# Last three slots of a two-layer decoder step: their output rows summed and written by themselves, the last down product in two banks of its own

## The chip, the cores and the metric

The kernel runs on one core of one Trainium2 chip. The metric is the device time of an execution in microseconds; a profiled execution also gives a trace.

## The reference, cut to what matters

A prompt group (512 tokens) and a sample group (64 tokens) go through two layers with shared weights, D = 1024. Each layer has a mixer (chunked gating and differential attention) and then a mixture of experts, which is what the change touches:

```python
def hier_moe(x, g2, r_g, r_e, w_gate, w_up, w_down):
    h = rmsnorm(x, g2).reshape(b * t, d)
    # group by argmax of softmax(h @ r_g); two experts of its four by softmax(h @ r_e)
    gates = ...                       # (tokens, 16), two non-zero
    hg = jnp.einsum('nd,edf->nef', h, w_gate)
    hu = jnp.einsum('nd,edf->nef', h, w_up)
    a = jax.nn.silu(hg) * hu * gates[..., None]
    return jnp.einsum('nef,efd->nd', a, w_down)
xp = xp + hier_moe(xp, ...)           # and the same for xs
```

The results are both x after layer 2, and the new key and value rows of both layers.

## The kernel before

**Tokens.** The tokens are five tiles of up to 128 rows (`NT`; tile `TP` = 4 has the 64 sample rows). Rows lie in `x` (SBUF). `h_rows` (DRAM) holds the normed rows; `y_rows` (DRAM) has 2 x 640 rows of expert results. Of a token's two experts, the one later in the order of places writes into the first 640 rows (main, or "higher"), the other into the second 640 ("lower").

**Slots.** The experts are worked off in 14 slots (`SLOTS`) of 128 token rows; slots 0 to 10 may mix experts, and slots 11, 12, 13 (`LAST` = 11) each hold one expert of the group's last places, so their rows are always main rows. Tokens that don't fit go to extra slots, whose number is read by every engine from `flags` at the end (`extra_slots`, `only_if`); here there are none. A slot n is: POOL gathers rows of `h_rows` (L634); TensorE transposes them (`turn_in`), VectorE scales them (`in_turned`, L1993); TensorE makes the gate and up products in two halves (`up`); ScalarE applies silu (L1375), VectorE multiplies (`gated`, L2007); TensorE turns the result (`turn_act`, bank J) and ScalarE copies it (`act_turned`, L1379); TensorE makes the down product (`down`, banks O, 4 x 2 matmuls of 512 columns); ScalarE copies it to `y_sb` (`result`, L1386); POOL scatters it to `y_rows` (`scatter`, L641).

**Order.** It is written out by hand. TensorE in step n: first half of up(n), turn_act(n-1), second half of up(n), turn_in(n+1), down(n-1). At the end come a flush and the branch on the extra slots. Every engine works its instructions in order, DMA issues too. In POOL's loop the gather of slot n+3 stands ahead of the scatter of slot n. SP issues all weight loads (L480), each when the buffer it takes is free; ten pieces of 1 MB are in SBUF.

**End of a layer.** While slots 12 and 13 run, ScalarE's queue loads the lower rows (`y_low`, L1401) and VectorE adds them to x with their gate (`add_low`, L1999), behind the gated products of these slots. Tokens whose lower row is in an extra slot have gate zero here (`late_gates`). When the scatters of all slots have landed, ScalarE's queue loads the main rows (`y_high`, L1417), VectorE adds them (`add_high`, also L1999), and in layer 1 SP stores x to the outputs (L498). In layer 0 TensorE does matmuls without use meanwhile (`keep_busy`, L713), 30 of them, of two passes each. The next layer starts with the transposes of x (`turn_input`, L695) and VectorE's scaling of them (L1473).

## Time and profile before

| | us |
|---|---|
| median of 3 runs (lowest, highest) | 998.91 (998.38, 1002.36) |
| profiled execution | 999.48 |
| its span | 997.8 |
| TensorE busy in it | 957.9 |
| VectorE, ScalarE, POOL busy | 457.8, 247.0, 193.6 |

The span goes from the first to the last instruction. TensorE is busy 96% of it; the 40 us that it isn't are mostly the end of layer 1 and, less, the end of layer 0. The DMA engines moved 197.5 MB, 198 GB/s over the span.

### The profile page before, as it was taken

Reading aid. Unit: us, or ns where it says so; the run is one execution under the profiler, and the core shown is the slowest. Engines: PE = TensorE matmul, PEld = TensorE weight load, DVE = VectorE, ACT = ScalarE, POOL = GpSimd, SP = SyncE. Lnnn points to the kernel's source line nnn. Section 1 sums busy time; section 2 is a strip of 40 time slices with the busy share of each in tenths; the row PEclk is TensorE's granted clock in tenths of the full one; section 3 lists DMA queues with packets and bytes.
Section 4 is the critical chain, followed back from the end, with each engine's and each line's share of the span. In section 5 each row is a group of like instructions: output and inputs, shape, how many; then the busy total and the mean of one; then the engine's idle time right before and its main releaser. Section 6 shows DMA issues by size and latency. Waiting matters only on the chain.

```text
span 997.8 us, 13511 instructions
## 1 busy us (share of the span) xinstructions
PE 957.9 (96%) x4838; PEld 489.5 (49%) x4838; DVE 457.8 (46%) x1210; ACT 247.0 (25%) x489; POOL 193.6 (19%) x267
## 2 busy tenths in 40 slices
PE   9999999999999999999899999999999999999991
PEld 5444455556456444434544445555565554444340
DVE  2403234676456665551433212456663575555523
ACT  3102355642001111111221124556220012111110
POOL 2333201331101111111124041023220012111100
PEclk9999999999999999999999999999999999999996
DMA  9706003342514979998651150135252168799946
GB/s 347 267 30 263 1 1 132 96 159 83 234 53 138 371 267 369 416 422 320 234 165 58 65 199 1 61 114 167 61 208 116 43 264 327 290 385 413 403 152 222
DMA packets 39769, 197.50 MB, mean 198 GB/s; under 512 B 7652, under 2 KB 7780, under 8 KB 23824
## 3 DMA queue, kind: packets, MB, share of 16 engines
q1 hardware_dynamic: 19456, 136.01, 34.9%
q0 software_dynamic: 15888, 45.79, 13.3%
q10 hardware_dynamic: 4352, 14.76, 4.0%
q8 instruction: 42, 0.69, 0.3%
q14 instruction: 31, 0.25, 0.1%
HBM read 177.22 MB, written 29.88 MB: 208 GB/s over the span
## 4 chain that ended last, share of the span: by engine, by line
PE 87%; DVE 5%; issue 3%; DMA 2%; ACT 1%; POOL 1%; POOLq 1%; ACTq 0%; DVEq 0%
PE ps L697 79%; PE ps L695 7%; DMA cat<-y_rows 1%; DMA y_rows<-hn,isca 1%; DVE cat L1852 1%; PE ps L713 1%; DMA hT<-h_rows,igat 1%; DVE hT L1993 0%; POOLq L526 0%; DVE hT L1473 0%; ACT hn L1386 0%; DVE x L1999 0%; DVE tmp L1559 0%; DVE tmp L1609 0%; POOL st L521 0%
## 5 line engine op out<-in xcount | busy, mean ns | idle before, releaser
L697 PE MATMUL ps<-ring,hT 128*128 128x512 f32 (+2 forms) x1056 | 382.7, 595 | 2.8 <-DVE hT L1473 1.6
L697 PEld LDWEIGHTS ps<-ring,hT 128*128 128x128 f32 (+2 forms) x1056 | 148.6, 166 | 195.5 <-issue 193.8
L697 PE MATMUL ps<-ring,cat 128*128 128x512 f32 (+2 forms) x560 | 195.3, 596 | 2.4 <-ACT hn L1386 2.4
L697 PEld LDWEIGHTS ps<-ring,cat 128*128 128x128 f32 (+2 forms) x560 | 72.9, 162 | 81.7 <-issue 78.8
L641 POOL DMA_INDIRECT y_rows<-hn,isca x28 | 29.2, 1044 | 249.0 <-ACT hn L1386 228.5
L697 PE MATMUL ps<-hT,ring 128*128 128x512 f32 (+1 forms) x256 | 71.8, 437 | 0.9 <-DVE tmp L1559 0.7
L521 POOL TENSOR_TENSOR st<-st,half 128x1 f32<-128x1 f32 (+3 forms) x60 | 63.5, 1058 | 11.3 <-POOL st L519 11.1
L1494 DVE TENSOR_REDUCE st<-sqj 128x8 f32<-128x512 f32 x20 | 13.5, 681 | 111.7 <-ACT sqj L1235 111.6
L519 POOL TENSOR_SCALAR st<-st 128x1 f32<-128x1 f32 (+3 forms) x60 | 15.1, 252 | 238.7 <-DVE st L1494 82.8
L1993 DVE TENSOR_TENSOR hT<-ps,par 128x512 f32<-128x512 f32 x56 | 36.2, 686 | 47.9 <-PE ps L695 47.1
L1386 ACT COPY hn<-ps 128x1024 f32<-128x1024 f32 x28 | 28.4, 1013 | 116.3 <-PE ps L697 116.3
L697 PEld LDWEIGHTS ps<-hT,ring 128*128 128x128 f32 x256 | 38.1, 191 | 30.5 <-issue 28.4
L527 POOL DMA_DIRECT2D kc<-in_ck x32 | 24.6, 770 | 102.3 <-PE ps L697 78.2
L1220 ACT ACTIVATE sqj<-x 128x1024 f32<-128x1024 f32 x10 | 10.6, 1058 | 119.6 <-DVE x L1686 99.1
L1307 ACT ACTIVATE ring<-ps,st 128x128 f32<-128x128 f32 (+3 forms) x64 | 33.2, 524 | 27.1 <-DVE st L1621 26.8
L1887 DVE TENSOR_REDUCE o_sb<-ps 128x4 f32<-128x12 f32 (+2 forms) x18 | 3.0, 164 | 80.1 <-PE ps L697 80.1
L1235 ACT ACTIVATE sqj<-ps,st 128x512 f32<-128x512 f32 (+1 forms) x20 | 13.7, 686 | 97.9 <-PE ps L697 91.3
L697 PE MATMUL ps<-vc,hT 128*128 128x512 f32 (+2 forms) x112 | 36.5, 598 | 0.9 <-issue 0.9
L634 POOL DMA_INDIRECT hT<-h_rows,igat x26 | 26.5, 1019 | 51.1 <-DVE isca L1891 44.9
L1473 DVE TENSOR_TENSOR hT<-ps,g_sb 128x512 f32<-128x512 f32 x20 | 12.9, 686 | 49.4 <-PE ps L695 49.4
L1375 ACT ACTIVATE cat<-ps 128x256 f32<-128x256 f32 x28 | 10.8, 385 | 97.6 <-PE ps L697 97.6
L527 POOL DMA_DIRECT2D vc<-in_cv x32 | 17.7, 552 | 87.9 <-PE ps L697 72.0
(269 smaller groups left out, 1219.4 us busy)
## 6 DMA issues: line engine op xcount, KB each, us to landing
ring<-in_w SPq DMA_DIRECT2D x82, 1024.0 KB, 8.3
kc<-in_w SPq DMA_DIRECT2D x12, 1024.0 KB
vc<-in_w SPq DMA_DIRECT2D x10, 1024.0 KB
v<-in_w SPq DMA_DIRECT2D x10, 1024.0 KB
kva<-in_w SPq DMA_DIRECT2D x10, 1024.0 KB
kc<-in_ck POOLq DMA_DIRECT2D x32, 256.0 KB, 3.7
vc<-in_cv POOLq DMA_DIRECT2D x32, 256.0 KB, 3.3
h_rows<-qk ACTq DMA_DIRECT2D x10, 512.0 KB, 2.6
```

The lines of the kernel that those rows point to most:

```text
L519: nc.gpsimd.tensor_scalar(stat["ms"][at, 0:n], src, 1.0 / size, EPS, ALU.mult, ALU.add).then_inc(*pool_c.inc())
L521: nc.gpsimd.tensor_tensor(dst, stat["ms"][at, 0:n], half[at, 0:n], ALU.pow).then_inc(*pool_c.inc(*label))
L527: pool.dma_start(buffer(b % 2, g), view(d[table][bass.DynSlice(l * NPOOL + page, 1)])).then_inc(*arrived[b % 2].inc("kv", b, by=16))
L634: pool.indirect_dma_start(hs[:, b, :], None, h_rows, bass.IndirectOffsetOnAxis(index, 0), bounds_check=TOK - 1, oob_is_err=False).then_inc ...
L641: pool.indirect_dma_start(rows, bass.IndirectOffsetOnAxis(index, 0), y_sb[:, b, :], None, bounds_check=rows.shape[0] - 1, oob_is_err=False ...
L695: ins = pe.transpose(out, lhsT, rhs)
L697: ins = pe.matmul(out, lhsT, rhs, start=start, stop=stop, skip_group_check=loose)
L1235: nc.scalar.activation(sqj[at, t % 2, :], bank(u)[at, :], ACT.Square, scale=stat["rs"][at, t:t + 1]).then_inc(*act_s.inc("sq", name, t))
L1307: ins = nc.scalar.activation(e_sb[:, n % 2, m, 0:(i + 1) * P], bank(f"S{n % 2}", m)[:, 0:(i + 1) * P], ACT.Exp, bias=stat["nb"][:, c:c + 1 ...
L1386: nc.scalar.copy(y_sb[:, b, :], ps[:, 6:8, :].rearrange("p a n -> p (a n)")).then_inc(*read["O"].inc("down", *key))
L1494: vec.tensor_reduce(stat["ssk"][:, 8 * t:8 * t + 8], groups(sqj[:, t % 2, :], 8, DK), AX.X, ALU.add).then_inc(*dve_s.inc("ss" + name, t))
L1993: vec.tensor_tensor(hsT[:, b, hf * HALF:(hf + 1) * HALF, :], bank(f"T{hf}").rearrange("p (j t) -> p j t", j=HALF), g, ALU.mult).then_inc(* ...
```

## The change

Only in layer 1 (`l == L - 1`):

- SP (`last_rows`), behind all weight loads: stores x to a new DRAM table `x_rows` (five stores), stores for each token a pair of gates to `g_rows` (five small stores), waits for the scatters of slots 9 and 10, loads the five tiles of lower rows to `y_low`, then, when the pieces through down(10) are free, the five tiles of main rows into freed weight buffers; stores each tile of x to the output when its sum is made (`dve_s "sum"`), waits for the three last scatters (`fin_out`), and only then reads the number of extra slots.
- POOL (`final_rows`), between the gather of slot 13 and the scatter of slot 10: waits for `x_rows` and `g_rows` and gathers, for slots 11, 12, 13, the rows of x and the gate pairs (six indirect gathers). Behind the scatter of slot 10 (`lower_rows`): waits for the scatters of 9 and 10 and gathers the three slots' lower rows. The scatters of slots 11 to 13 to `y_rows` are gone (they stand in the branch for extra slots); instead `final_out` scatters the summed rows to the output, after all main stores have landed.
- VectorE: small operations for the gates in slot 5 (`final_gates`); gate zero for main rows that the last slots will write themselves. Behind the gated product of slot 12: wait for `x_rows`, five `add_low`, `add_main` for tiles 0 and 1. Behind that of slot 13: `add_main` for tiles 2 to 4, `slot_lower` and `slot_higher` for the three slots. For slot 13 `slot_higher` reads the down product from PSUM in two halves.
- ScalarE no longer loads `y_low` or `y_high` when there are no extra slots.

In both layers: `turn_act` of slot 13 is done between the two halves of down(12) and ScalarE copies it ahead of the result of slot 12; down(13) goes into banks J and I, and ScalarE copies the halves one by one. `keep_busy` is 32 instead of 30 between the layers, and 5 at the start of both layers instead of 6 at the start of layer 0 alone. The outputs of both groups are one tensor, and at the start one more block of 64 rows of `y_rows` is zeroed.

```diff
+                def last_rows():
+                    for t in range(NT):
+                        sp.dma_start(x_rows[PLACE[t] * P:(PLACE[t] + 1) * P, :], x[:, t, :]).then_inc(*x_kept.inc("x", by=16))
+                    sp.wait_ge(*dve_s.at("pairs"))
+                    for t in range(NT):
+                        sp.dma_start(g_rows[PLACE[t] * P:(PLACE[t] + 1) * P, :], g_pair[:, t, :]).then_inc(*g_kept.inc("g", by=16))
+                    for b in range(2):
+                        sp.wait_ge(*y_out[b].at("y", "m", last_slot(b, LAST)))
+                    for t in range(NT):
+                        sp.dma_start(y_low[:, t, :], y_rows[TOK + PLACE[t] * P:TOK + (PLACE[t] + 1) * P, :]).then_inc(*lower_in[t].inc("early", by=16))
+                    sp.wait_ge(piece_used.sem, l * PER_LAYER + (N_DENSE + FIN_FREE + CREDIT))
+                    for t in range(NT):
+                        n = NROW if t == TP else P
+                        sp.dma_start(y_main(t)[0:n, :], y_rows[PLACE[t] * P:PLACE[t] * P + n, :]).then_inc(*main_in[t].inc("main", by=16))
+                    for t in range(NT):
+                        sp.wait_ge(*dve_s.at("sum", t))
+                        sp.dma_start(d["y"][PLACE[t] * P:(PLACE[t] + 1) * P, :], x[:, t, :]).then_inc(*stored.inc("main", by=16))
+                    sp.wait_ge(*fin_out.at("fin"))
...
+                def final_rows():
+                    wait(*x_kept.at("x"))
+                    wait(*g_kept.at("g"))
+                    wait(*pool_c.at("g_slot"))
+                    for i, n in enumerate(FIN):
+                        for out, table, landed in ((x_slot[n], x_rows, xg_in[i]), (g_slot[:, i, :], g_rows, gg_in[i])):
+                            pool.indirect_dma_start(out, None, table, bass.IndirectOffsetOnAxis(igat[:, n:n + 1], 0),
+                                                    bounds_check=TOK - 1, oob_is_err=False).then_inc(*landed.inc("in", by=16))
+                def lower_rows():
+                    for b in range(2):
+                        wait(*y_out[b].at("y", "m", last_slot(b, LAST)))
...
+                        pool.indirect_dma_start(yg_slot[n], None, y_rows, bass.IndirectOffsetOnAxis(ilow[:, i:i + 1], 0),
+                                                bounds_check=2 * TOK - 1, oob_is_err=False).then_inc(*yg_in[i].inc("in", by=16))
+                def final_out(n):
+                    wait(*dve_s.at("fin", n))
+                    wait(*stored.at("main"))
+                    pool.indirect_dma_start(d["y"], bass.IndirectOffsetOnAxis(igat[:, n:n + 1], 0), x_slot[n], None,
+                                            bounds_check=TOK - 1, oob_is_err=False).then_inc(*fin_out.inc("fin", by=16))
                 for n in range(NSLOT):
                     if n + 3 < NSLOT:
                         gather_main(n + 3)
+                    if l == L - 1 and n == LAST - 1:
+                        final_rows()
...
-                    scatter(n % 2, isca[:, n:n + 1], ("m", n), y_out[n % 2])
+                    if l < L - 1 or n < LAST:
+                        scatter(n % 2, isca[:, n:n + 1], ("m", n), y_out[n % 2])
+                    if l == L - 1 and n == LAST - 1:
+                        lower_rows()
+                if l == L - 1:
+                    for n in FIN:
+                        final_out(n)
...
-                    keep_busy(30, "I")
+                    keep_busy(32, "I")
...
-                                if l == 0:
-                                    keep_busy(6, "I")
+                                keep_busy(5, "I")
...
+                    out = ("J", "I") if key == ("m", NSLOT - 1) else ("O",)
+                    for u in out:
+                        claim(u)
...
+                        if between and c == 0:
+                            between()
...
                     gated(n % 2, ("m", n))
+                    elif n == NSLOT - 2:
+                        dve.wait_ge(*x_kept.at("x"))
+                        for t in range(NT):
+                            add_low(t)
+                        add_main(0)
+                        add_main(1)
+                    elif n == NSLOT - 1:
+                        for t in range(2, NT):
+                            add_main(t)
+                        for work in (slot_lower, slot_higher):
+                            for m in FIN:
+                                work(m)
```

## Rows read from the trace of the kernel before

**Rows 1.** Busy time by stage: start:end, length, engines busy (operations), granted clock, DMA share, GB/s
```profile
core 0: us, PE busy (x) PEld busy (x) DVE busy (x) ACT busy (x) POOL busy (x), PEclk, DMA share, GB/s
900.00:920.00 20.00, 20.00 (x74) 7.94 (x70) 10.24 (x32) 3.15 (x5) 4.05 (x4) 1.00 1.02 414
980.00:998.00 18.00, 0.00 (x0) 0.00 (x0) 6.29 (x5) 0.00 (x0) 0.00 (x0) 0.50 0.76 277
```
**Rows 2.** The chain that ended last, from 961: start, length, what
```profile
973.29 3.69 PE ps L697 x8
...
977.00 1.02 ACT hn L1386
...
978.88 3.44 DMA y_rows<-hn,isca
...
982.39 0.32 ACTq L1417
...
983.71 7.47 DMA cat<-y_rows
...
991.20 1.28 DVE x L1999
```
**Rows 3.** Timeline of slots 12 and 13: start, length, operation [idle before, releaser]
```profile
957.51 1.29 DVE L1993 TENSOR_TENSOR hT<-ps,par 128x512 f32<-128x512 f32 x2 [9.93 <-PE ps L695]
...
968.27 3.60 PE L697 MATMUL ps<-kc,cat 128*128 128x512 f32 x8
...
968.89 0.42 DVE L2007 TENSOR_TENSOR cat<-cat,ps 128x256 f32<-128x256 f32 x1 [9.76 <-ACT cat L1375]
...
973.29 3.67 PE L697 MATMUL ps<-ring,cat 128*128 128x512 f32 x8 [1.20 <-ACT hn L1386]
```
**Rows 4.** SP's last weight issue, SP's waits for landed weights (L163), and that stretch
```profile
939.58 0.33 SPq L480 DMA_DIRECT2D ring<-in_w  x1
...
L163 SPq EVENT_SEMAPHORE  x5: 17/17/17, 953.2 to 953.5; - x5
...
950.00:953.20 3.20, 3.20 (x8) 1.28 (x7) 0.00 (x0) 0.83 (x1) 1.01 (x1) 1.00 0.24 99
```
**Rows 5.** DMA issues of the page: count, KB each, median us from issue to landing
```profile
h_rows<-qk ACTq DMA_DIRECT2D x10, 512.0 KB, 2.6
...
g_sb<-in_g ACTq DMA_DIRECT2D x1, 8.0 KB, 2.4
```
**Rows 6.** Timeline of POOL around the scatter of slot 10
```profile
939.43 1.01 POOL L641 DMA_INDIRECT y_rows<-hn,isca  x1 [9.80 <-ACT hn L1386]
940.74 1.01 POOL L634 DMA_INDIRECT hT<-h_rows,igat  x1 [0.31 <-issue]
951.71 1.01 POOL L641 DMA_INDIRECT y_rows<-hn,isca  x1 [9.96 <-ACT hn L1386]
```
**Rows 7.** Timeline of VectorE, adds of the reloaded main rows (tiles 0, 1; tile 2)
```profile
986.04 2.53 DVE L1999 SCALAR_TENSOR_TENSOR x<-cat,st,x 128x1024 f32<-128x1024 f32 x2 [9.53 <-DMA cat<-y_rows]
...
989.53 1.28 DVE L1999 SCALAR_TENSOR_TENSOR x<-cat,st,x 128x1024 f32<-128x1024 f32 x1 [0.95 <-DMA cat<-y_rows]
```
**Rows 8.** Stretch after the short gaps between the layers (columns as rows 1)
```profile
489.00:492.00 3.00, 3.00 (x18) 3.00 (x17) 0.00 (x0) 0.00 (x0) 0.00 (x0) 0.57 0.19 62
```
**Rows 9.** Timeline from the last down product of layer 0 to the first product of layer 1
```profile
482.07 3.67 PE L697 MATMUL ps<-ring,cat 128*128 128x512 f32 x8 [1.21 <-ACT hn L1386]
...
485.78 1.01 ACT L1386 COPY hn<-ps 128x1024 f32<-128x1024 f32 x1 [3.81 <-PE ps L697]
...
487.88 8.56 PE L713 MATMUL ps<-c 128*128 128x128 f32 x60 [2.03 <-issue]
...
495.17 2.54 DVE L1999 SCALAR_TENSOR_TENSOR x<-cat,st,x 128x1024 f32<-128x1024 f32 x2 [8.26 <-DMA cat<-y_rows]
...
499.18 1.10 PE L697 MATMUL ps<-ring,hT 128*128 128x512 f32 x2 [1.57 <-DVE hT L1473]
```
**Rows 10.** SP's load of the number of extra slots: durations ns, start
```profile
L430 SPq TENSOR_LOAD <-flags x1: 276/276/276, 940.0 to 940.0; - x1
```

More of the change, by code:

```diff
@@ L326, in program @@
         y_outx = [count(f"y_outx{b}") for b in range(2)]
+        x_kept, g_kept, fin_out = count("x_kept"), count("g_kept"), count("fin_out")
+        stored_again = count("stored_again")
+        main_in, lower_in, x_again = ([count(f"{n}_in{t}") for t in range(NT)] for n in ("main", "lower", "x_again"))
+        xg_in, gg_in, yg_in = ([count(f"{n}_in{i}") for i in range(3)] for n in ("xg", "gg", "yg"))
         early_in, low_in, high_in = ([count(f"{n}_in{t}") for t in range(NT)] for n in ("early", "low", "high"))
@@ L343, in program @@
         LOW_AT = {LAST + 1: (0, 1), LAST + 2: (2, 3, 4)}
+        FIN = tuple(range(LAST, NSLOT))
+        assert len(FIN) == 3 and all(len(SLOTS[n]) == 1 and SLOTS[n][0][1:] == (0, P) for n in FIN)
         def last_slot(b, below=NSLOT):
@@ L491, in load @@
                                      ).then_inc(*landed[SLOT[i]].inc("w", i, by=16))
-                extras(sp, n_extra, load, arrivals=landed)
-            for t in range(NT):
-                n = NROW if t == TP else P
-                sp.wait_ge(x_ready.sem, L * NT + t + 1)
-                sp.dma_start(d["ys"] if t == TP else d["yp"][t * P:(t + 1) * P, :], x[0:n, t, :]).then_inc(*stored.inc(by=16))
-            sp.wait_ge(stored.sem, stored.now())
+                extras(sp, n_extra, load, done=store_again if l == L - 1 else None, arrivals=landed, uncounted=[stored_again])
+            sp.wait_ge(*stored.at("main"))
             sp.wait_ge(*v_stored.at("v"))
@@ L637, in scatter @@
                 def scatter(b, index, key, landed):
-                    wait(*read["O"].at("down", *key))
+                    for u in ("J", "I") if key == ("m", NSLOT - 1) else ("O",):
+                        wait(*read[u].at("down", *key))
                     rows = y_rows[0:TOK, :] if key[0] == "m" and key[1] >= LAST else y_rows
-                    pool.indirect_dma_start(rows, bass.IndirectOffsetOnAxis(index, 0), y_sb[:, b, :], None,
+                    result = y_last if l == L - 1 and key == ("m", NSLOT - 1) else y_sb[:, b, :]
+                    pool.indirect_dma_start(rows, bass.IndirectOffsetOnAxis(index, 0), result, None,
                                             bounds_check=rows.shape[0] - 1, oob_is_err=False).then_inc(*landed.inc("y", *key, by=16))
@@ L675, in next_in @@
                         gather(b, rows_at(igat, 2, 0), (key, b), hs_inx[b])
+                    if l == L - 1 and (key, b) == ("e", 0):
+                        for n in FIN:
+                            scatter(n % 2, isca[:, n:n + 1], ("m", n), y_out[n % 2])
                     wait(*read["O"].at("down", key, b))
@@ L1140, in down @@
                             for at, i in parts:
[L1141 to L1142 removed]
+                                u, k = (out[c], 0) if len(out) == 2 else ("O", c)
+                                mm(bank(u, k)[at, :], actT[:, b, f, at], piece(i)[:, f * D + c * W:f * D + (c + 1) * W], start=(f == 0), stop=(f == 1),
+                                   inc=full[u].inc("down", *key) if ((c or len(out) == 2) and f and at.stop == P) else None)
+                        if between and c == 0:
+                            between()
                 def weights(n, part):
@@ L1426, in load_again @@
                     scattered_mains()
+                    if l == L - 1:
+                        act.wait_ge(*stored.at("main"))
+                        for t in range(NT):
+                            act.dma_start(x[:, t, :], x_rows[PLACE[t] * P:(PLACE[t] + 1) * P, :]).then_inc(*x_again[t].inc("x", by=16))
                     for t in range(NT + 2):
@@ new lines, in add_main, with slot_lower @@
+                def add_main(t):
+                    n = NROW if t == TP else P
+                    dve.wait_ge(*main_in[t].at("main"))
+                    vec.scalar_tensor_tensor(x[0:n, t, :], y_main(t)[0:n, :], stat["main"][0:n, t:t + 1], x[0:n, t, :], ALU.mult, ALU.add
+                                             ).then_inc(*dve_s.inc("sum", t))
+                def slot_lower(n):
+                    i = FIN.index(n)
+                    for arrived in (xg_in[i], gg_in[i], yg_in[i]):
+                        dve.wait_ge(*arrived.at("in"))
+                    vec.scalar_tensor_tensor(x_slot[n], yg_slot[n], g_slot[:, i, 1:2], x_slot[n], ALU.mult, ALU.add).then_inc(*dve_s.inc("lower", n))
@@ new lines, in slot_higher @@
+                def slot_higher(n):
+                    i = FIN.index(n)
+                    dve.wait_ge(*dve_s.at("lower", n))
+                    if n < NSLOT - 1:
+                        dve.wait_ge(*read["O"].at("down", "m", n))
+                        vec.scalar_tensor_tensor(x_slot[n], y_sb[:, n % 2, :], g_slot[:, i, 0:1], x_slot[n], ALU.mult, ALU.add).then_inc(*dve_s.inc("fin", n))
+                        return
+                    for c, u in enumerate(("J", "I")):
+                        dve.wait_ge(*full[u].at("down", "m", n))
+                        cols = x_slot[n][:, c * W:(c + 1) * W]
+                        ins = vec.scalar_tensor_tensor(cols, bank(u), g_slot[:, i, 0:1], cols, ALU.mult, ALU.add)
+                    ins.then_inc(*dve_s.inc("fin", n))
```

110 lines of the change are left out of this document (89 added, 21 removed).

## The prediction

> **What bounds the kernel now.** Read first the busy time by stage: until about 970 TensorE is busy all the time at full clock (20.00 of 20.00 us), and in the last stage, 980 to 998, it does nothing while VectorE has 6.29 us of work and the DMA engines are 0.76 busy [rows 1]. So everything up to 970 is worth what TensorE saves, and the last 28 us are worth what their own chain of waits costs. That chain [rows 2]: the last down product starts at 973.29, ScalarE copies it out (977.00), the scatter to y_rows takes until 982.32, the first reload of y_rows is issued at 982.39, the fourth is waited for until 991.18, VectorE adds, x is stored, and the span ends at 997.8. From the copy's end (978.02) that is 19.8 us of moving rows. The timeline of the last two slots shows the second thing: TensorE waits 1.2 us between slots 12 and 13, for bank O and the turned activations, and VectorE, after the gated product of slot 12, sits idle 9.76 us until that of slot 13 at 968.89 [rows 3].
>
> The change takes the 19.8 us apart, and puts into the idle time of VectorE, POOL and the DMA engines around 940 to 969 what has to be ready sooner. The question is whether that fits ahead of the two things it is queued in front of: on POOL the scatter of slot 10, on VectorE the gated product of slot 13, for which TensorE waits. I work in the times of the trace of before.
>
> **Layer 1, x into DRAM.** SP issues the five stores of x after its last weight load, issued at 939.58 [rows 4]. They go behind it in the same queue. SP's own wait for the landing of the last weights is over at 953.2: by then few DMA engines still work (99 GB/s from 950 to 953.2, against 414 in the steady stream), and all 16 must finish each transfer [rows 1, 4]. Each engine has 1/16 of 2.62 MB to go, at 414 GB/s 6.3 us: 959.5. A lone store of 512 KB takes 2.6 us to landing [rows 5], 1.3 of them beyond its bytes; five tiny stores of gates follow. I take 1.0 for both: x and gates are there at 960.5. Lower end: the engines idle from 950 to 953.2 have by then moved (414 - 99) x 3.2 = 1.0 MB of it, 2.4 us less, and nothing for the rest: 957. Upper end: 2.4 us for the tiny stores, as for the lone 8 KB load [rows 5], and stores a fifth slower than loads: 963.5.
>
> The Trainium skill (DMA: Bandwidth & Descriptors, section "Queues, rings and completion order") says that each DMA engine takes one issuer's descriptors in ring order. That is what keeps x behind the weights; the trace agrees in so far as the wait for the last weights ends with the late engines at 953.2; without the rule the lower end, 957 or less, would be the value.
>
> **Layer 1, POOL.** After the gather for slot 13 (940.74) POOL now waits for x and the gates and issues six gathers (x and gates, three slots), and only then the scatter of slot 10. Before, that scatter began at 951.71 [rows 6]. POOL takes 0.9 us from a release to the start of such an operation (copy's end 978.02, scatter 978.88 [rows 2]), and scatter and gather follow one another at 1.31 us. So 960.5 + 0.9 + 6 x 1.31 = 969.3 for the scatter, 17.6 us late, with 3.4 to landing [rows 2] 972.7. Lower end of the six: 1.01 each, the operation alone, 6.1; upper end: 1.31, as nothing here queues longer.
>
> **Layer 1, the reloads.** The loads of the lower rows (five, SP) wait for the scatter of slot 10, the loads of the main rows (five) follow them on SP, and POOL's three gathers of lower rows start at the same moment. VectorE must have the five lower and two main tiles before the gated product of slot 13. The first lands 3.65 us after issue (982.39 to 986.04) [rows 2, 7]. Six loads and the three gathers are between it and the seventh: nine pieces of 512 KB. Between the first and the fourth of before (986.04, 991.18) lie 5.14 us, 1.7 each, with stores beside them; the bare bytes at 414 GB/s take 1.27. I take 1.42: 972.7 + 3.65 + 12.8 = 989.1; ends 11.4 and 15.4 for the nine.
>
> A formula of the Trainium skill (the same page, section "Anatomy of one DMA") gives a fixed 2.0 us plus bytes over 436 GB/s; as an estimate from the page the ten pieces would take 2.0 + 12.0 = 14.0 us against my 16.4, and everything behind would be 2.4 us earlier. Its 436 is shown by no stretch here; the streams show 414.
>
> **Layer 1, VectorE from there.** One add of a main tile 1.28 (the last of its two ahead of the gated product), the gated product 0.41, three main adds 3.84, three lower adds for the slots 3.84, the adds of slots 11 and 12 2.57, and slot 13 in two halves from PSUM, each at 0.65 (half of 1.29 for the two 128x512 reads of PSUM) 1.3 [rows 2, 3, 7]: 13.2 us, 1002.3. TensorE, meanwhile, stands since 970.0 (half of the down product of slot 12 that starts at 968.27) until the gated product at 990.8. It comes back at a low clock: after the short gaps at the end of layer 0 the granted clock was 0.57 from 489 to 492 [rows 8]. Half a down product and a whole one, 1.7 and 3.4 at full clock [rows 3], are 10.3 at half all through, plus the turn: 1001.7, and 0.65 for the last half. So even at its worst TensorE ends with VectorE, and at its best 4 us sooner; I add nothing, 0.3 at the upper end. The turn inside the product ahead and the two banks thus save their 1.2 us in layer 1 for nobody.
>
> **The end.** The scatter of slot 13 starts 0.87 after the add and lands in 3.44 (978.02 to 982.32, [rows 2]): 1006.6. The main stores and the scatters of slots 11 and 12 are issued 2 us and more before and hidden. SP now goes through its branch on the extra slots after the last landing; its load of the flag alone is 0.28 [rows 10], with the register work and the semaphores behind it I take 1.3 (0.7 to 2.0), and the 0.4 that lay between landing and span's end before. 1008.3.
>
> **Layer 0.** There the last three slots stay as they are, but the turn and the banks count. TensorE's wait of 1.21 at 482.07 goes; ScalarE copies the first half while the second is multiplied, so its result is complete some 0.6 (half of 1.01 and a little) after the product instead of 1.01. Scatter and reload come 1.8 us earlier, and x of tile 0 with them (495.17) [rows 9]. TensorE's filling work grows from 60 passes to 64, at 8.56/60 us each 0.6 us more, and starts 1.2 earlier. What is late next is that filling and VectorE's turned tile: the first product of layer 1 (499.18) comes 1.2 earlier. The five matmuls put in ahead of it are ten passes, 1.1 to 1.4 us in a gap of 1.57 before [rows 9]; without cover they cost up to 1.2 and nothing is gained. At the kernel's start there are two passes less, 0.2. I take 1.4 off, ends 0 and 1.9. The nine small operations for the gates in slot 5 lie in VectorE's idle half (10.24 busy of 20 [rows 1]); even 3 us of them would end ahead of the next turned rows. The extra blank store and the memset are long before anyone waits. All taken as nothing.
>
> **Sum.** 1008.3 - 1.4 = 1006.9, plus 1.7 outside the span (999.48 for the execution, 997.8 for its span), 1008.6 for an execution of this kind; the profiled one is 0.6 above the median of its runs (998.91), so 1008.0. With all lower ends (957, 6.1, 11.4, 0.7 at the end, 1.9 in layer 0) it is 1000; with all upper ones 1016. The engines idle before 953.2 speak for the lower end of the first term more than anything does for its upper one; for that I take 1 off and say 1007.
>
> **The rivals.**
> A. POOL isn't held: x lands while the weights still stream, and the scatter of slot 10 keeps its 951.71, or nearly. Rows at 955.1, the seventh load at 955.1 + 16.45 = 971.5, VectorE to 984.8, end 990.8, less 1.4 and by the same terms as above 990.5: faster by 8. For it: POOL idles 10 us there and the DMA engines are half idle from 946 on. Against: the stores stand behind all weights still under way. The point from which it decides is the landing of x and the gates: 951.71 less 0.9 and 7.9 is 943, each microsecond after it is one at the end, and at 951 the gain of 8 is used up; the last weights alone land at 953. Chance 0.18.
> B. The same, and the reloads are there before VectorE asks: then VectorE starts from the gated product at 969.3, ends 13.2 - 1.28 - 0.41 later, and the median would be 986.5. Against: 5 MB must pass in 14 us beside gathers. Chance 0.06.
> C. The forecast's chain, but with cheap queues (gathers at 1.01, loads at the bare rate): 1000 to 1003, no change to be seen. Chance 0.14.
> Forecast: 0.62.
>
> A measurement of this kernel tells 0.5% (5 us) from no change. Slower (over 1003.9) 0.62, same 0.14, faster 0.24. The likeliest case alone has 1002 to 1014; the range that holds 8 in 10 reaches into A: 990 to 1013.
>
> **What would show it.** In the profile after: a gap of TensorE in the middle of the down product of slot 12, some 18 us; the scatter of slot 10 after six gathers, near 969 (less 1.4); VectorE idle from the gated product of slot 12 until the lower rows come; a VectorE chain of nine adds behind the gated product of slot 13. The forecast is wrong if that scatter starts ahead of 955, or if VectorE's adds of lower rows end before slot 13 is up.

## The result

| | before | after |
|---|---|---|
| median of 6 runs each, one chip (lowest, highest), us | 999.61 (998.38, 1002.42) | 1015.27 (1013.09, 1017.64) |
| profiled execution, us | 999.48 | 1014.21 |
| its span, us | 997.8 | 1012.2 |
| mean granted TensorE clock | 0.989 | 0.982 |
| scatter of slot 9 to the span's end, us | 58.4 | 71.8 |

The ratio is 1.0136, with a 95% interval of 1.0118 to 1.0154: slower by 1.4%. The direction was forecast, and so was the mechanism; the time was not. 1007 us was said, with 1013 as the upper end, and 1015.3 was measured.

The scatter of slot 9 is the last event that both kernels do alike. Most of what follows is measured from there: the 14.4 us between the two spans are 13.4 behind it and 0.95 ahead of it.

POOL's timeline of the kernel after answers [rows 6]. The columns are start, us busy, engine, line, operation, and in brackets the idle time before it and what ended that:

```profile
940.38 1.02 POOL L695 DMA_INDIRECT y_rows<-hn,isca  x1 [9.80 <-ACT hn L1496]
941.70 1.02 POOL L686 DMA_INDIRECT hT<-h_rows,igat  x1 [0.30 <-issue]
964.07 0.99 POOL L712 DMA_INDIRECT ws<-x_rows,igat  x1 [21.36 <-DMA g_rows<-g_pair]
965.37 1.00 POOL L712 DMA_INDIRECT g_slot<-g_rows,igat  x1 [0.30 <-issue]
...
971.89 1.01 POOL L695 DMA_INDIRECT y_rows<-hn,isca  x1 [0.30 <-issue]
976.18 1.02 POOL L723 DMA_INDIRECT cat<-y_rows,ilow  x1 [3.28 <-issue]
...
1006.49 0.98 POOL L730 DMA_INDIRECT out_y<-hT,igat  x1 [0.30 <-issue]
```

POOL stands 21.36 us for the landing of the gates, then issues its six gathers, and the scatter of slot 10 starts at 971.89. In the kernel before it started at 951.71. SP's timeline, same columns, which answers [rows 4]:

```profile
940.53 0.74 SPq L505 DMA_DIRECT2D ring<-in_w  x1
941.31 2.59 SPq L510 DMA_DIRECT2D x_rows<-x  x5
943.94 7.75 SPq L513 DMA_DIRECT2D g_rows<-g_pair  x5
975.16 2.30 SPq L517 DMA_DIRECT2D qk<-y_rows  x5
977.50 3.00 SPq L521 DMA_DIRECT2D ring<-y_rows  x5
990.41 7.70 SPq L524 DMA_DIRECT2D out_y<-x  x5
```

The ten stores follow the last weight load at once. The lower rows are asked for at 975.16, the moment the scatter of slot 10 has landed. VectorE's timeline, which answers [rows 3, 7]:

```profile
959.67 0.41 DVE L2164 TENSOR_TENSOR cat<-cat,ps 128x256 f32<-128x256 f32 x1
978.47 2.64 DVE L2156 SCALAR_TENSOR_TENSOR x<-qk,st,x 128x1024 f32<-128x1024 f32 x2 [18.39 <-DMA qk<-y_rows]
...
990.57 1.29 DVE L2089 SCALAR_TENSOR_TENSOR x<-ring,st,x 128x1024 f32<-128x1024 f32 x1 [0.19 <-DMA ring<-y_rows]
991.77 0.41 DVE L2164 TENSOR_TENSOR cat<-cat,ps 128x256 f32<-128x256 f32 x1
992.89 1.28 DVE L2089 SCALAR_TENSOR_TENSOR x<-ring,st,x 128x1024 f32<-128x1024 f32 x1 [0.71 <-DMA ring<-y_rows]
995.27 2.47 DVE L2089 SCALAR_TENSOR_TENSOR x<-ring,st,x 128x1024 f32<-128x1024 f32 x2 [1.10 <-DMA ring<-y_rows]
...
1003.65 1.40 DVE L2108 SCALAR_TENSOR_TENSOR hT<-ps,g_slot,hT 128x512 f32<-128x512 f32 x2
```

VectorE idles 18.39 us where it idled 9.76, and the gated product of slot 13 is made at 991.77 (968.89 before). TensorE's timeline has the gap that was forecast in the middle of the down product of slot 12:

```profile
969.23 1.88 PE L792 MATMUL ps<-kc,cat 128*128 128x512 f32 x4
992.24 0.69 PE L790 MATMUL ps<-c,cat 128*128 128x128 f32 x2 [21.13 <-DVE cat L2164]
992.72 3.62 PE L792 MATMUL ps<-kc,cat 128*128 128x512 f32 x4
996.13 4.09 PE L792 MATMUL ps<-ring,cat 128*128 128x512 f32 x8
```

It looks like the whole loss, 21.13 us of the busiest engine; the fourth experiment shows that it costs nothing that the runs can tell. The chain that ended last (start, us, what) runs past it, from one wait on a transfer to the next:

```profile
950.77 12.37 DMA g_rows<-g_pair
...
971.89 3.25 DMA y_rows<-hn,isca
...
979.01 16.24 DMA ring<-y_rows
995.27 0.34 DVE x L2089
```

### The profile page after: what moved, and what is told of

It is laid out like the page before. It is cut to its first block, busy times and chain, and to the rows that moved or that the text cites. A ratio compares the mean times of both kernels' runs of the same rounds, so it can differ in the third digit from the quotient of the medians.

```text
span 1012.2 us, 13611 instructions
## 1 busy us (share of the span) xinstructions
PE 961.6 (95%) x4850; PEld 491.6 (49%) x4850; DVE 466.5 (46%) x1226; ACT 247.4 (24%) x491; POOL 203.1 (20%) x278
## 4 chain that ended last, share of the span: by engine, by line
PE 82%; DVE 6%; DMA 5%; issue 3%; SPq 1%; POOL 1%; POOLq 1%; ACT 1%; DVEq 0%; ACTq 0%
PE ps L792 75%; PE ps L790 7%; DMA ring<-y_rows 2%; DMA g_rows<-g_pair 1%; DMA y_rows<-hn,isca 1%; SPq L513 1%; DMA hT<-h_rows,igat 1%; DVE cat L1968 1%; PE ps L808 1%; DVE hT L2150 0%; POOLq L576 0%; DVE hT L1589 0%; DMA cat<-y_rows 0%; DVE tmp L1675 0%; DVE tmp L1725 0%
## 5 line engine op out<-in xcount | busy, mean ns | idle before, releaser
L792 PE MATMUL ps<-hT,ring 128*128 128x512 f32 (+1 forms) x256 | 71.8, 437 | 0.9 <-DVE tmp L1675 0.7
L695 POOL DMA_INDIRECT y_rows<-hn,isca x25 | 25.7, 1029 | 214.3 <-ACT hn L1496 182.2
L1496 ACT COPY hn<-ps 128x1024 f32<-128x1024 f32 x26 | 26.3, 1013 | 107.0 <-PE ps L792 107.0
L790 PE MATMUL ps<-c,cat 128*128 128x128 f32 (+1 forms) x96 | 16.4, 278 | 21.2 <-DVE cat L2164 21.1
## 6 DMA issues: line engine op xcount, KB each, us to landing
kc<-in_w SPq DMA_DIRECT2D x12, 1024.0 KB, 10.7
v<-in_w SPq DMA_DIRECT2D x10, 1024.0 KB, 12.4
```

What stands on the lines that cost most here:

```text
L695: pool.indirect_dma_start(rows, bass.IndirectOffsetOnAxis(index, 0), result, None, bounds_check=rows.shape[0] - 1, oob_is_err=False).then_ ...
L790: ins = pe.transpose(out, lhsT, rhs)
L792: ins = pe.matmul(out, lhsT, rhs, start=start, stop=stop, skip_group_check=loose)
L1496: nc.scalar.copy(y_sb[:, b, :], ps[:, 6:8, :].rearrange("p a n -> p (a n)")).then_inc(*read["O"].inc("down", *key))
```

## The experiments

Each was timed beside the kernel before on its chip. As the section is read from one execution each, differences of 3 us in it tell nothing: x_quiet has 2.6 more than x_quiet_gates_wide and the lower ratio. "Section" is the time from the scatter of slot 9 to the span's end in the one profiled execution.

| kernel | ratio to before (95%) | span | section | scatter 10: start | to its landing | seventh tile added from |
|---|---|---|---|---|---|---|
| before | 1 | 997.8 | 58.4 | 951.71 | | |
| after | 1.0136 (1.0118, 1.0154) | 1012.2 | 71.8 | 971.89 | 3.3 | 990.57 |
| banks_only | 0.9971 (0.9952, 0.9989) | 993.3 | 56.5 | 949.12 | | |
| pool_after | 1.0049 (1.0033, 1.0065) | 1007.1 | 64.5 | 954.95 | 10.1 | 984.30 |
| x_early | 1.0067 (1.0042, 1.0092) | 1005.6 | 58.4 | 961.91 | 5.4 | 985.25 |
| gated_first | 1.0115 (1.0077, 1.0153) | 1013.9 | 73.3 | 972.60 | 3.7 | 993.94 |
| x_quiet | 0.9991 (0.9973, 1.0008) | 1002.5 | 61.4 | 953.40 | 10.7 | 981.77 |
| x_quiet_gated_first | 0.9990 (0.9971, 1.0008) | 1001.1 | 60.1 | 953.28 | 9.6 | 980.00 |
| gates_wide | 1.0129 (1.0105, 1.0154) | 1012.8 | 70.1 | 972.25 | 3.3 | 991.85 |
| x_quiet_gates_wide | 1.0017 (1.0001, 1.0034) | 1000.3 | 58.8 | 953.74 | 8.6 | 980.39 |
| x_quiet_gates_wide_first | 1.0006 (0.9989, 1.0023) | 1001.3 | 59.5 | 954.11 | 8.2 | 980.46 |
| x_quiet_pool_after | 1.0004 (0.9988, 1.0020) | 1002.5 | 60.0 | 954.80 | 6.5 | 980.48 |

The landing is read at the issue of SP's first load of lower rows, which waits for it. In x_quiet_gates_wide and x_quiet_gates_wide_first SP waits 0.8 and 0.5 us longer, for the gates; there it is read at the last of the sixteen increments by which the trace records the end of a transfer (there are 16 DMA engines). In the kernel before and in banks_only those give 3.3 us for the same scatter.

**1. The turn and the banks alone** (banks_only), in the kernel before:

```diff
-                    keep_busy(30, "I")
+                    keep_busy(32, "I")
-                down(1 - b, ("m", n - 1), weights(n - 1, 2))
+                down(1 - b, ("m", n - 1), weights(n - 1, 2), last_turn if n == NSLOT - 1 else None)
+                out = ("J", "I") if key == ("m", NSLOT - 1) else ("O",)
```

> The kernel before with only the part of the change that both layers share: the turn of slot 13 inside the down product of slot 12, the last down product in banks J and I, 32 filling matmuls between the layers and 5 at the start of each. No rows are kept or gathered. Theory: layer 0 ends 1.5 us earlier as in the profile after (first product of layer 1 at 497.7 instead of 499.2) and layer 1 ends 1.8 earlier, so 996.3 without anything else. The profile after had a stretch at half clock at 731 in the mixing of layer 1, which cost 1.6 us and which the profile before did not have. If it belongs to this part it is here too and the time is about 997.9; a ratio of 0.997 to 0.999. Rival: the lost 2.4 us between 498 and 940 come from the added small work for the gates and from its transfers, then nothing is lost here and the time is 996, with the same point of layer 1 (the scatter of slot 9, 939.43 before, 940.38 after) at 937.9.

Measured: 0.9971, a gain, the only one of the study: 998.3 against 1001.7 in the same runs. Its timeline of TensorE has no gap where the kernel before has 1.20 us [rows 3]:

```profile
965.69 1.88 PE L698 MATMUL ps<-kc,cat 128*128 128x512 f32 x4
967.40 0.38 PE L696 MATMUL ps<-c,cat 128*128 128x128 f32 x2
967.62 1.88 PE L698 MATMUL ps<-kc,cat 128*128 128x512 f32 x4
969.34 3.60 PE L698 MATMUL ps<-ring,cat 128*128 128x512 f32 x8
```

Two readings follow. This part of the change is good for 0.3%, so everything else in it costs 1.65%. And the section shrinks from 58.4 to 56.5 us, as it should where the end hangs on the last down product (1.9 us by itself is within what one execution can tell); in the kernel after the end does not hang on it, and the same saving goes to nobody.

**2. The six gathers behind the scatter of slot 10** (pool_after). The scatter no longer waits for x and gates:

```diff
-                    if l == L - 1 and n == LAST - 1:
-                        final_rows()
                     ...
                         lower_rows()
+                        final_rows()
```

> The kernel after with the six gathers of x and gates moved on POOL behind the scatter of slot 10 and the gathers of lower rows; stores of x still behind the weights. Theory (two things hold VectorE's adds: POOL's order, and the landing of x and gates at 963.2): the scatter of slot 10 starts at 952.7 instead of 971.9, but the loads of lower rows are queued behind the stores of x and gates and VectorE waits for x, so the first add starts at about 963.5 instead of 978.5, the gated product of slot 13 comes at 977 to 979 instead of 991.8, and the span is some 13 us shorter: 998 to 1001, device time 1000 to 1002. If POOL's order alone were the cause, the first add would start at 959.5 and the time would be 994 to 996. If neither is (the volume of reloads is), the time stays above 1008.

Measured: 1.0049. The place of the six gathers in POOL's queue was the larger part of the loss: 7.3 us of the section, 0.87% of the time. The rest of what was expected did not come, since the scatter, on time at 954.95, took 10.1 us to land where it had taken 3.3:

```profile
946.49 8.34 SPq L513 DMA_DIRECT2D g_rows<-g_pair  x5
965.06 2.52 SPq L517 DMA_DIRECT2D qk<-y_rows  x5
```

**3. The stores of x and gates among the weight loads** (x_early), ahead of loads 32 and 39:

```diff
+                    if l == L - 1 and i == 32:
+                        ... # the five stores of x
+                    if l == L - 1 and i == 39:
+                        sp.wait_ge(*dve_s.at("pairs"))
+                        ... # the five stores of gates
```

> The kernel after with POOL's order kept, but the five stores of x issued in the quiet stretch of the weight stream ahead of weight load 32 (about 844 to 856) and the five of the gates ahead of load 39. Theory: both are there when POOL asks, its six gathers run from 943 to 951, the scatter of slot 10 starts at 952.7, the first add at 959.5, the gated product of slot 13 at 972 to 973, and the span ends 18 to 19 us earlier than after: 993 to 995, device time 995 to 997, ratio to before 0.994 to 0.998. Rival (the 2.6 MB more in a stream that is nearly full delay the weights): TensorE waits for weights between 858 and 950, the scatter of slot 9 comes 3 to 6 us later than 940.4, and the time is 1000 or more. Rival (the reload of 6 MB is the bound whatever comes before): the time stays above 1005.

Measured: 1.0067. The section is short, 58.4, as long as before; what was lost lies ahead of it, as the first rival said. Waits of the kernel x_early from 915 to 945 (engine, what, for what: total us, times, longest):

```profile
PE ps L794 <- DMA ring<-in_w: 4.9, 3, 2.6
```

its five stores of gates on SP, and its windows (us, then the busy time of each engine, the clock, the DMA share, GB/s):

```profile
878.48 2.23 SPq L500 DMA_DIRECT2D g_rows<-g_pair  x5
...
884.00:896.00 12.00, 12.00 (x40) 5.65 (x37) 3.26 (x9) 1.77 (x3) 2.02 (x2) 1.00 0.99 288
...
932.00:942.00 10.00, 6.70 (x48) 2.83 (x50) 4.32 (x12) 0.54 (x2) 0.00 (x0) 0.93 1.01 419
```

The same stretch in the kernel after:

```profile
884.00:896.00 12.00, 12.00 (x40) 5.58 (x37) 3.90 (x11) 1.77 (x3) 2.02 (x2) 1.00 1.01 408
```

The DMA engines are at their limit there [rows 1], and 30 us later TensorE waits 4.9 us for weights. The scatter of slot 9 starts at 947.24, 6.9 later than in the kernel after. Two things take the time. The 2.62 MB of x are 6.3 us at 414 GB/s, less what fell into idle time. And from 884 to 896, where the gates' rows of 8 bytes are among the weights, the engines are as busy and move 1.4 MB less than in the kernel after, 3.5 us at the same rate: by the trace's records of single packets the 8 KB packets of the weights took 439 ns each there, against 321. How much of the 6.9 each of the two is was not separated.

**4. The gated product of slot 13 ahead of all adds** (gated_first). TensorE's gap goes, the rows come no sooner:

```diff
-                    elif n == NSLOT - 2:
+                    elif n == NSLOT - 1:
                         ... # five add_low
-                        add_main(0)
-                        add_main(1)
-                    elif n == NSLOT - 1:
-                        for t in range(2, NT):
+                        for t in range(NT):
                             add_main(t)
```

> The kernel after with one thing moved on VectorE: all adds of lower and main tiles stand behind the gated product of slot 13, so TensorE never waits for them. POOL's order and SP's stores are as in the kernel after. Theory (the end is set by rows landing late and by VectorE's row of adds, TensorE's stand of 21 us costs nothing): TensorE is done near 980, the fifth lower tile is added at 987, the last main tile lands at 995, and VectorE ends at 1004.6 instead of 1005.1: span 1011 to 1012.5, ratio to before 1.012 to 1.015. Rival (the stand of TensorE, and its half clock after it, is what costs): the product of slot 13 comes 20 us sooner and the time falls by 8 to 12 us, to 1003.

Measured: 1.0115, the same as the kernel after within the intervals. VectorE's timeline:

```profile
970.11 0.42 DVE L2164 TENSOR_TENSOR cat<-cat,ps 128x256 f32<-128x256 f32 x1 [9.76 <-ACT cat L1476]
981.46 2.61 DVE L2156 SCALAR_TENSOR_TENSOR x<-qk,st,x 128x1024 f32<-128x1024 f32 x2 [10.94 <-DMA qk<-y_rows]
...
1005.53 1.40 DVE L2108 SCALAR_TENSOR_TENSOR hT<-ps,g_slot,hT 128x512 f32<-128x512 f32 x2
```

The product is made at 970.11 and no row of TensorE has an idle time behind it, and still the last add is at 1005.53 and the span ends at 1013.9. So the 21 us of TensorE are a symptom; the two ratios are 2 us apart, and their intervals leave room for up to 6; experiment 6, with a gap of 12 us, narrows that. The end is set by rows landing and VectorE's adds.

**5. Stores of x right behind weight load 31, and the gates gathered late** (x_quiet), issued at 844.71, ten us sooner than in experiment 3, when the weights that TensorE needs next are already on their way:

```diff
+                    if l == L - 1 and i == 31:
+                        ... # the five stores of x
                     def final_rows():       # now the three gathers of x alone
+                    def gate_rows():        # the three of gates, behind lower_rows()
```

> The kernel after with the stores of x issued right behind weight load 31 (844, before the quiet 846 to 858), the stores of gates where they were, behind the weights, and POOL split: three gathers of x ahead of the scatter of slot 10, three of gates behind the gathers of lower rows. Theory: x takes nothing from the weights, so TensorE doesn't wait in the stream (4.9 us in x_early) and the scatter of slot 9 stays at 938 to 941; the scatter of slot 10 starts 12.3 later, its rows land in 3.4, and the seventh reloaded tile 16 to 18 us behind them, the gated product of slot 13 stands 3 to 5 us. From the scatter of slot 9 to the end 54 to 56 us (before 58.4, after 71.8, x_early 58.4): span 993 to 996, ratio 0.995 to 0.999. Rival (2.6 MB more delay the weights wherever they stand): TensorE waits for weights about 5 us near 920 to 941, as in x_early, and the ratio is 1.002 or more.

Measured: 0.9991, no difference from before, and 14.5 us better than the kernel after by the ratios. TensorE waits for no weights, and POOL's gathers of x start without a wait:

```profile
943.75 0.99 POOL L710 DMA_INDIRECT ws<-x_rows,igat  x1 [0.30 <-issue]
...
953.40 1.01 POOL L696 DMA_INDIRECT y_rows<-hn,isca  x1 [6.06 <-ACT hn L1503]
965.27 1.02 POOL L729 DMA_INDIRECT cat<-y_rows,ilow  x1 [10.86 <-issue]
```

The window from 848 to 860, a pause in the weight stream, tells where x went:

```profile
848.00:860.00 12.00, 12.00 (x107) 5.15 (x109) 8.28 (x30) 1.73 (x4) 2.02 (x2) 1.00 0.96 352
```

The kernel after moves 144 GB/s in it and x_early 203. So x_quiet puts 2.5 MB more through the pause, nearly all of x, and x_early 0.7. Without the hold of the scatter the loss against the kernel before is gone. But the scatter lands 10.7 us after its start, as in experiment 2, and the gain that the change was laid out for doesn't come either.

**6. Both together** (x_quiet_gated_first): the edits of 5 and 4.

> Both: x_quiet and all adds behind the gated product of slot 13. Theory: TensorE has no gap, the adds of the five lower tiles start 9 us later than in x_quiet (969 instead of 960) and VectorE's row of adds, 10 for tiles and 7 for slots at 1.2 us, is the bound from there: 970 + 20.3 + 7.2, 997 to 998, 2 to 4 us longer than x_quiet. Rival (landings bound, VectorE waits between adds anyway): the same as x_quiet within 1 us.

Measured: 0.9990. The order of VectorE's work makes no difference here either: the rival, within about 2.5 us by the intervals.

**7 to 9. Rows of gates of 512 bytes instead of 8** (gates_wide; x_quiet_gates_wide with the edits of 5; x_quiet_gates_wide_first with those of 5 and 4). The suspicion was that 640 packets of 8 bytes hold the DMA engines in front of the scatter:

```diff
-    g_rows = nc.dram_tensor("g_rows", [TOK, 2], F32).ap()
+    g_rows = nc.dram_tensor("g_rows", [TOK, 128], F32).ap()
+        g_pair = qk[:, 0:NT * 128].rearrange("p (t n) -> p t n", t=NT)
+        g_slot = tmp[:, 0:384].rearrange("p (i c) -> p i c", i=3)
...
+                    sp.wait_ge(*g_kept.at("g"))     # SP, ahead of the loads of lower rows
```

The wider rows of gates lie in `qk`, where the lower rows will land, so SP has to wait for the gates' stores before it loads those: a second change, which comes with the first.

> The kernel after with gate rows of 512 bytes instead of 8 and nothing else. Theory: the small packets, queued behind x, also hold back x's own last packets on slower engines: x and gates are there at 960 instead of 963.2 and the time falls by 3 us, ratio 1.010 to 1.011. Rival (x alone is the bound, its fifth store landed at 962.3): the time falls by less than 1 us.

> x_quiet with one thing changed: the gates are stored and gathered in rows of 512 bytes instead of 8 (the pair is the first two of 128 numbers). In x_quiet the five gate stores stood in the DMA queues from 942 to 963, at 145 GB/s and half the engines' share, and the scatter of slot 10 took 10.7 us to landing, against 3.3 before and 5.4 in x_early, whose gate stores came earlier. Theory (640 packets of 8 bytes hold the engines and what lands beside them): with wide rows the scatter lands in 3.4 to 4.5, everything behind it comes 6 to 7 us sooner, from the scatter of slot 9 to the end 54.5 to 56 us instead of 61.4, ratio to before 0.992 to 0.994. Rival (the ten reloads and three gathers in 18 us are slow by themselves and the scatter's landing is absorbed): 59 to 61 us and a ratio of 0.997 to 0.999.

> x_quiet_gates_wide with all adds behind the gated product of slot 13. Theory: with rows there at 957 the VectorE row of adds is the bound, and starting it at 970 instead of 960 costs it 3 to 6 us: 57 to 61 us from the scatter of slot 9 to the end, ratio 0.996 to 0.999. Rival (landings bound it): within 1 us of x_quiet_gates_wide.

Measured: 1.0129, 1.0017 and 1.0006, each beside its twin with small rows (1.0136, 0.9991, 0.9990) with no gain in time. The sections of the profiled executions are 1.7, 2.6 and 0.6 us shorter than the twins', which is within what one execution tells. In the two kernels with the edits of 5 the two changes pull against each other. The scatter lands 2.1 and 1.4 us sooner than in the twins (8.6 and 8.2 us), and then SP's new wait holds the loads, here in x_quiet_gates_wide:

```profile
SPq L519 <- DMA g_rows<-qk: 0.8, 1, 0.8
```

The records of single packets show what the small rows do: from 950 to 952 an 8 KB packet of the weights took 539 ns on the mean beside rows of 8 bytes (x_quiet) and 309 beside rows of 512 (x_quiet_gates_wide). So the suspicion was right as to what happens, and wrong as to its weight: it is 2 of the 7 us by which the landing is late, and a gain in time is not shown. Windows of x_quiet_gates_wide:

```profile
952.00:956.00 4.00, 4.00 (x12) 1.80 (x12) 0.00 (x0) 1.19 (x2) 1.01 (x1) 1.00 0.62 243
956.00:960.00 4.00, 4.00 (x17) 2.25 (x16) 0.46 (x1) 0.43 (x2) 0.00 (x0) 1.00 0.45 176
960.00:964.00 4.00, 4.00 (x10) 1.71 (x9) 1.16 (x3) 0.58 (x1) 0.50 (x1) 1.00 0.10 35
```

While the scatter is under way the engines are on the mean half idle, and at the end nine tenths. Its sixteen increments tell that some are done and others behind: in x_quiet eight came within 3.3 us, as on quiet engines, seven after 6.7 to 8.4, and the last alone after 10.7; with wide rows eight came within 2.6, the last after 8.6.

**10. x early, all six gathers late** (x_quiet_pool_after): the stores of experiment 5 with the order of experiment 2. Nothing but weights and gates is left in front of the scatter.

> The change with two steps moved: the five stores of x go behind weight load 31, and all six gathers (x and gates) go behind the scatter of slot 10 and the gathers of lower rows. So neither the x stores nor the x gathers lie in the last 12 us of the weight stream, in front of that scatter; only the five gate stores stay there. Theory (the scatter of slot 10 took about 10 us to land in x_quiet, pool_after and x_quiet_gates_wide, because transfers put into the still full DMA engines were ahead of its rows): here it starts near 953 and lands in 3.3 to 4.5 us, SP issues the lower reloads near 957 to 958 (964.1 in x_quiet), VectorE's first add comes near 961 to 962, and from the scatter of slot 9 to the span's end it is 54 to 57 us (x_quiet 61.4, before 58.4); ratio to before 0.993 to 0.996. Rival: the tail of the weights and the gate stores alone hold the rows; then the scatter lands 9 us or more after its start all the same, the lower reloads are issued at 962 or later, and the ratio is 0.998 to 1.001. Second rival: the scatter lands early, but the six gathers and the ten reloads together use up the DMA engines, so the last slots' sums end as late as in x_quiet: lower reloads before 958, ratio still 0.998 or more.

Measured: 1.0004. The landing took 6.5 us, between the figures of theory and rival:

```profile
954.80 1.01 POOL L696 DMA_INDIRECT y_rows<-hn,isca  x1 [9.96 <-ACT hn L1496]
962.30 1.01 POOL L724 DMA_INDIRECT cat<-y_rows,ilow  x1 [6.50 <-issue]
...
974.47 1.00 POOL L713 DMA_INDIRECT g_slot<-g_rows,igat  x1 [0.30 <-issue]
```

So transfers put in front of the scatter are a good part of its landing: without the 1.5 MB of gathers it is 4 us shorter than in x_quiet (10.7 to 6.5). Of the 3 us that are left above the 3.3 of the kernel after, the gates' stores are the likely cause, though no run takes them alone away. The kernel before has the weights' tail in front of its scatter too, and it lands in 3.3; here the last packet of the weights starts 16.8 us after its issue (12.8 in the kernel before), and their 8 KB packets took 803 ns each from 952 to 954. What the second rival describes is seen as well, though not its condition (reloads before 958; they are issued at 961.29): the six gathers now share the engines with the reloads, the seventh tile is ready 19.2 us after their issue (15.4 in the kernel after), and the 4 us are gone again.

The last two main tiles say why no order of this work beat the kernel before. They are added from 995.27 in the kernel after, 990.40 in pool_after, 985.77 in x_quiet, 985.85 in x_quiet_pool_after and 983.64 in x_quiet_gates_wide, and the span ends 16.9, 16.7, 16.7, 16.7 and 16.7 us later. To end by the 997.8 of before they would have to be there by 981. Behind the scatter of slot 10 thirteen pieces of up to 512 KB must pass first, and in no order did the last of them come earlier than 20 us after that scatter had landed (975.16 to 995.27 in the kernel after, 964.14 to 985.77 in x_quiet).

The version to keep is banks_only: it beats the kernel before by 0.3% and the kernel after by 1.6%.

## Why the prediction was right and wrong

Right was the chain: stores behind the weights, POOL held, the scatter of slot 10 after six gathers, VectorE's idle time in front of the lower rows, the adds behind the gated product. The rivals A and B (POOL isn't held) are ruled out by the 21.36 us of the timeline; C (cheap queues) by the six gathers at 1.3 each, though its loads came nearly true: the nine pieces took 12.1 us (978.47 to 990.57), 1.34 each. That TensorE's gap costs nothing was said, and experiments 4 and 6 agree.

What failed is the size of four terms of the sum, not a link of the chain: the 1.4 us taken off for layer 0 (slot 9 came 0.95 later instead), the 1.0 us for x's last bytes and the gates (2.7 measured, for which another 1.0 had been taken off the total), VectorE's row of adds (14.5 us instead of 13.2) and the end (7.15 instead of 6.0). The forecast's span of 1006.9 against 1012.2, term by term:

| term | forecast | measured | more, us |
|---|---|---|---|
| start of the scatter of slot 9, against before | -1.4 | +0.95 | +2.35 |
| from there to x and gates in DRAM | 21.1 | 22.8 | +1.7 |
| POOL to the scatter of slot 10, and its landing | 12.2 | 12.0 | -0.2 |
| reload to the seventh tile | 16.45 | 15.4 | -1.0 |
| VectorE to the last add | 13.2 | 14.5 | +1.3 |
| last scatter and SP's end | 6.0 | 7.15 | +1.1 |

That is 5.3. The other 3.0 of the 8.3 between 1007 and 1015.3 lie outside the trace: 1.0 that I took off the sum by choice, and 2.0 by which the median stands further above the span (3.1) than reckoned (1.1). Of these, 1.7 are the luck of which execution was profiled: it was 0.6 above the median of its three runs in the kernel before, and is 1.1 below that of its six here.

- **Layer 0 and the front.** The gain at the layer boundary is there as worked out, 1.5 us: down(13) starts at 480.95 with no gap, and the first product of layer 1 at 497.67 (499.18 in [rows 9]). It is lost on the way. Windows of the kernel after:

```profile
489.00:492.00 3.00, 3.00 (x29) 3.00 (x28) 0.00 (x0) 0.00 (x0) 0.00 (x0) 1.00 0.29 85
...
731.00:734.00 3.00, 3.00 (x37) 2.56 (x39) 1.36 (x2) 0.00 (x0) 0.00 (x0) 0.50 0.02 5
```

  and of the kernel before, in the mixer of layer 1:

```profile
731.00:734.00 3.00, 3.00 (x56) 2.71 (x58) 2.04 (x2) 0.38 (x2) 0.00 (x0) 1.00 0.02 5
```

  The kernel before has its stretch at half clock (1.2 GHz) at 489 to 492 [rows 8]; the kernel after has it at 731, where it costs 1.6 us, 37 matmuls in 3 us where 56 went at full clock (2.4 GHz): the same VectorE operations come 1.21 us ahead of the kernel before at 730 (730.32 to 731.53) and 0.40 behind it at 735 (735.53 to 735.13). From 728 to 731 TensorE was busy 1.97 of 3 us in the kernel after, and 1.53 in the kernel before, whose clock stayed up. Banks_only has neither, pool_after and gated_first both. The step "I take 1.4 off" read a clock of one execution as a property of the code. Another 0.6 is lost at the start of the experts, where TensorE waits for the first gathered rows, here in the waits of the kernel after from 800 to 830 (0.3 in the kernel before):

```profile
PE ps L790 <- DMA hT<-h_rows,igat: 0.9, 1, 0.9
```

   The added operations of VectorE in slot 5 cost nothing that shows, as said: from 830 to 950 TensorE has no wait for VectorE.
- **Landing of x and gates.** 1.7 short. The sum had x's bytes through at 959.5 and took 1.0 for what x needs beyond them and for the gates. The fifth store of x, issued at 943.37, was there after 18.9 us, at 962.3; less the 0.95 by which everything is later, that is 1.8 behind 959.5. The last of the gates, 12.4 us after its issue (the chain above), was there 0.9 behind x, though the five took SP 7.75 us to issue, 3.17 of it one of them. So the larger part of the error is x's own landing, and the rows of 8 bytes seem to be in it too: in gates_wide x is there 19.7 us after the start of slot 9's scatter (962.39 less 942.69), in the kernel after 21.9, by the sum 20.1; and from 956 to 958 a 4 KB packet took 284 ns on the mean in the kernel after, 159 in gates_wide. The microsecond taken off the sum, because engines idled before 953.2, had the wrong sign.
- **Reload.** 15.4 against 16.45, inside its two ends; this error hid 1.0 of the others.
- **VectorE.** The adds were counted without waits; VectorE waited 0.71 us for the third main tile and 1.10 for the fourth.
- **The end.** The scatter of slot 13 started 1.44 behind the last add (1005.05 to 1006.49), third in POOL's line at 1.3 us a scatter, and not 0.87: the two ahead of it were called hidden and weren't. Its landing and SP's branch then took 5.7 us instead of 5.1.

The sum's upper end of 1016 held the 1015.3. The range given did not reach to it, although the terms of the queues (x, gates, the end) came from transfers that stood nearly alone in their queues, which was a reason to lean to their upper ends.

## What to carry to other kernels

Ask of a wait that is added to a queue what is behind it: one place in POOL's order cost 7 us here (experiment 2), more than twice the 3 us that the turn and the banks gained. A gap of the busiest engine is a loss only if the end hangs on it; making it go (experiment 4) tells in one run. And work moved into "idle" time ahead of a small transfer has to be charged with that transfer's landing, which went from 3.3 to 10 us, even where it doesn't delay its issue. Very small rows in a full stream are to be charged with more than their bytes.

## What the runs showed of the hardware

- A scatter of 512 KB lands in 3.3 us on quiet DMA engines (after) and also with nothing but the end of the weight stream in front of it (before, banks_only); with stores or gathers of the change in front of it, it took 5.4 to 10.7 us (x_early, x_quiet), at a mean busy share of the engines of 0.1 to 0.6 in x_quiet_gates_wide. The mean hides that some engines are done and others behind: in x_quiet eight of the sixteen increments came within 3.3 us and the last after 10.7; in pool_after they are spread from 2.8 to 10.1 us. The Trainium skill (DMA: Bandwidth & Descriptors, section "Queues, rings and completion order") says that each DMA engine goes round between the rows it has work for, packet by packet. By that POOL's scatter should have had its turns beside the stores on SP's queue in pool_after; it took 10.1 us all the same. Whether the rule fails there or a few engines are slow for another reason stays open, as the trace doesn't say which engine an increment is from.
- Rows of 8 bytes slow the large packets beside them: the 8 KB packets of the weights took 439 ns beside them in x_early from 884 to 896 (321 in the kernel after) and 539 ns in x_quiet from 950 to 952, against 309 beside rows of 512 bytes in x_quiet_gates_wide. The kernel's time did not tell: 1.0136 with rows of 8 bytes and 1.0129 with rows of 512.
- The half-clock stretches of TensorE, 1.6 us for the one at 731 in the kernel after, fall at other places in other executions: at 489 (before), at 731 (after), at both (pool_after, gated_first) or at neither (banks_only, x_early), though the code around 731 is the same in all. After its stand of 21.13 us in the kernel after TensorE had a granted clock of 0.50 from 992.20 to 996.20, and four matmuls took 3.62 us that take 1.88 at full clock.
- SP issues a store in 0.5 us, and took up to 3.17 for one of gates behind the last weights and x in the kernel after. Chain of that kernel:

```profile
944.68 0.51 SPq L513
945.23 3.17 SPq L513
```
